# First block of a three-block fp32 transformer kernel: the low parts of weight quarters one batch later, the forget gates' logarithm and the value tiles in another order and other PSUM banks, squares added on VectorE

## The chip, the cores and the metric
One core of a Trainium2 chip runs the whole program. The metric is device time in microseconds (us) of one execution. A trace is taken of one further execution; its span, from the first to the last instruction, is a little shorter than its device time.

## The reference, cut to what matters
512 tokens with 16 meta tokens ahead of them go through one first block and two hybrid layers, all in float32. The change is in the first block:

```python
hn = rms_norm(h, ln_pre_mix)                     # (528, 1024)
proj = hn @ w_in
q_a, k_a, v_a, q_b, k_b, v_b, f_b = ...          # 8 heads each, k_a and v_a 2 heads
o_a = swa_sink_attention(q_a, k_a, v_a, sinks, rel_bias)      # window of 128 and the meta tokens, T5 bias
o_b = forgetting_attention(q_b, k_b, v_b, f_b + b_forget)     # logit[t,s] += sum of log sigmoid(f), s < j <= t
h = h + rms_norm(concat(o_a, o_b) @ w_out, ln_post_mix)
hn = rms_norm(h, ln_pre_ffn)
h = h + rms_norm((silu(hn @ w_gate) * (hn @ w_up)) @ w_down, ln_post_ffn)
```

Two hybrid layers (latent attention, two convolution branches, a gated merge) follow and are the longer part of the time.

## The kernel before, in words
**Products in three parts.** Each float32 matrix x is split into a high part (rounded to fp32r) and a low part (the rest), and a product is three matmuls (`mm3`, L602: high*high, low*high and high*low). Weights come as 134 slots of 128 x 2048 numbers (1 MB), loaded in order by the SP queue into three buffers (L480 to L486); a load waits until the slot three before it is used up (`slot_done`). ScalarE writes the high part (`slot_hi`, L1188), VectorE the low part (`slot_lo`, L1635), each either whole or in quarters of 512 columns, and TensorE waits for both (`split_ready`, L613). All helpers for ScalarE's activations record line 1186, VectorE's record L1626 (tensor with tensor), L1630 and L1633.

**Order.** Each engine's order of work is written out by hand, and the engines meet at counting semaphores. The PSUM has eight banks of 512 columns; banks 0 and 1 are handed on by `bank_read` counters (`Fills`, L165; `wait_fill`, L595).

**First norm** (L701 to L706, L1243 to L1256, L1695 to L1722). ScalarE squares the eight tiles of x, VectorE adds them into `acc`, and TensorE sums over partitions with `acc` against a column of ones (`token_sums`, L644). The last two squares are not added but summed by TensorE too (its argument `late`). The root, its reciprocal on a diagonal (`token_roots`) and `spread` (L659) bring the factor to all partitions; VectorE then scales x and splits it.

**Projections of the first block.** Slot 0: keys and values of the windowed part, and the forget logits beside it. Slots 1 and 2: the keys of the forgetting part (`keys_tile`, L683), two tiles a slot in banks 0 and 1 or 2 and 3; between their halves TensorE makes eight rows of the bias table (`bias_row`, L667) in banks 4 and 5, which ScalarE copies to `brow` (L1231); GpSimd writes them to DRAM and reads them back skewed. Between the two tiles of slot 1 the logits are turned (L739 to L743). VectorE adds the gate's bias (`fx`), ScalarE takes abs, exp(-x) and ln(1+x) (L1294 to L1299, with a load of activation tables before the second and the third), VectorE makes `ls`, and TensorE sums it up by triangular products (L772 to L779). Slots 3 and 4: the values, four tiles of 128 tokens in banks 2 to 5 and one tile of the meta tokens in bank 0 (L754 to L769), copied by VectorE (`v_read`, L1776) and ScalarE (`Vm`, L1312). Slot 5: queries of heads 0 to 3 in banks 0 and 1 (L781), copied to `Qb` by `queries_read`.

**Attention** (L909 to L918). 32 batches: two blocks of 128 queries of one head each, 16 of the forgetting part and then 16 of the windowed part. In iteration j TensorE transposes the probabilities of batch j, does some *dense steps*, then the scores of batch j+2 and the values product of batch j. ScalarE in iteration j: exponentials of j+1, the copy of the transposed batch j, reads of dense tiles, a quarter of a slot's high part (L1372 to L1381). VectorE: norm of j (`normed`), maxima of j+1, and the low part of the same quarter (L1826 to L1836). A dense step is one k of one tile of slots 6 to 10 (3 matmuls of 512 columns): 80 steps in all; `dense_until(j)` (L135) says how many are through after batch j. `SPLITS` (L161) says in which iteration which quarter of slots 7 to 12 is split. Banks 2 to 5 hold scores, 6 and 7 the outputs.

**Second norm** (L924 to L956, L1386 to L1396, L1840 to L1872). Slots 11 and 12 end the output projection in eight tiles; VectorE adds each to `y1` (the trace calls that memory `y`), ScalarE squares it, GpSimd adds up the squares 0 to 6 (`add_up`, L561) between the loads of the adaptation weights that it issues, and TensorE sums and spreads (`token_sums(1, ...)`). Meanwhile slots 13 and 14 (`S_GU`, `S_GU + 1`) are split.

## Time and profile before

| | us |
|---|---|
| median of 3 runs (1864.39 to 1869.49) | 1867.81 |
| the profiled execution: its own time | 1867.15 |
| its span | 1865.2 |
| mean granted TensorE clock | 0.979 of full |
| HBM traffic, mean over the span | 94 GB/s |

TensorE's busy time stands in the rows below. Engines are PE (TensorE), PEld (its weight loads, beside PE), DVE (VectorE), ACT (ScalarE), POOL (GpSimd) and SP (the DMA queue). Times of rows are microseconds from the start of the span, unless marked ns. A matmul row's duration reaches beyond the start of the next one, since they are pipelined; the distance of two starts is what one costs.

### The profile page before, as it was taken

The page shows a single profiled execution, that of the slowest core. Times are in us where ns is not written, and L with a number is a line of the kernel's source. Part 1 is how long each engine was busy: PE and PEld are TensorE (multiplying, and loading weights), DVE is VectorE, ACT ScalarE, POOL GpSimd, SP SyncE. Part 2 cuts the span into 40 slices and gives each one's busy share as a digit, 9 for nine tenths or more (in the row PEclk, how much of TensorE's full clock was granted, in tenths as well). Part 3 has the DMA queues.
Part 4 walks back from the last instruction along what each step waited for, and adds up shares of the span by engine and source line. Part 5 has one row for each costly group of instructions (what it writes and reads, how often), then busy time and mean ns, then how long its engine had stood idle before and what let it go on. Part 6 is the DMA issues. An engine that isn't in the chain of part 4 may idle for free.

```text
span 1865.2 us, 20425 instructions
## 1 busy us (share of the span) xinstructions
PE 1783.6 (96%) x8186; PEld 1425.2 (76%) x8186; DVE 1062.8 (57%) x1724; ACT 689.0 (37%) x1056; POOL 117.1 (6%) x120
## 2 busy tenths in 40 slices
PE   8999998999999999999899999999999999999996
PEld 7766766788888887777788788777777778788775
DVE  6344443776665336634368766557543458766555
ACT  4425454422222234464423322532455422322432
POOL 2100001011000000100000000021100000000002
PEclk8999999999999999999999999999999999999998
DMA  4220012265554321211122222221321112222221
GB/s 163 106 102 24 23 46 82 85 208 204 200 181 164 130 91 68 90 69 68 46 90 91 90 91 103 78 90 46 113 91 49 65 68 91 90 91 90 91 90 46
DMA packets 29532, 177.40 MB, mean 95 GB/s; under 512 B 3613, under 2 KB 3757, under 8 KB 12286
## 3 DMA queue, kind: packets, MB, share of 16 engines
q1 hardware_dynamic: 20448, 144.71, 21.6%
q0 software_dynamic: 8608, 31.21, 4.8%
q8 instruction: 64, 1.05, 0.2%
q10 hardware_dynamic: 382, 0.19, 0.0%
q14 instruction: 30, 0.25, 0.0%
HBM read 171.28 MB, written 4.78 MB: 94 GB/s over the span
## 4 chain that ended last, share of the span: by engine, by line
PE 72%; DVE 6%; ACT 3%; issue 1%; POOL 1%; DMA 0%; DVEq 0%; POOLq 0%
PE ps L603 22%; PE ps L605 22%; PE ps L604 22%; PE ps L1106 2%; PE ps L1091 2%; DVE w_lo L1626 2%; DVE h L1626 1%; PE ps L1097 1%; DVE R L1670 1%; ACT w_hi L1186 1%; POOL acc L524 1%; ACT h L1186 1%; DVE cacc L1633 1%; DVE tmp L1626 0%; DVE ps L2024 0%
## 5 line engine op out<-in xcount | busy, mean ns | idle before, releaser
L603 PE MATMUL ps<-Xh,w_hi 128*128 128x512 f32 (+1 forms) x1664 | 657.0, 395 | 23.8 <-DVE w_lo L1626 9.3
L604 PE MATMUL ps<-Xl,w_hi 128*128 128x512 f32 (+1 forms) x1664 | 642.5, 386 | 0.0
L605 PE MATMUL ps<-Xh,w_lo 128*128 128x512 f32 (+1 forms) x1664 | 642.4, 386 | 0.0
L1626 DVE TENSOR_TENSOR w_lo<-w_raw,w_hi 128x2048 fp32r<-128x2048 f32 (+1 forms) x161 | 312.4, 1942 | 348.8 <-ACT w_hi L1186 348.8
L603 PEld LDWEIGHTS ps<-Xh,w_hi 128*128 128x128 f32 x1664 | 315.4, 190 | 99.2 <-issue 24.4
L1186 ACT ACTIVATE w_hi<-w_raw 128x2048 fp32r<-128x2048 f32 (+1 forms) x155 | 259.7, 1678 | 304.8 <-DMA w_raw<-in_w 278.6
L604 PEld LDWEIGHTS ps<-Xl,w_hi 128*128 128x128 f32 x1664 | 315.7, 190 | 65.3 <-issue 4.8
L605 PEld LDWEIGHTS ps<-Xh,w_lo 128*128 128x128 f32 x1664 | 315.4, 190 | 63.2
L1633 DVE SCALAR_TENSOR_TENSOR cacc<-ain,vec,cacc 128x512 f32<-128x512 f32 x240 | 161.9, 748 | 0.0
L1186 ACT ACTIVATE gt<-ps 128x512 f32<-128x512 f32 x48 | 28.2, 597 | 205.4 <-PE ps L605 205.3
L605 PE MATMUL ps<-act_h,w_lo 128*128 128x512 f32 x176 | 70.2, 399 | 0.0
L604 PE MATMUL ps<-act_l,w_hi 128*128 128x512 f32 x176 | 69.4, 394 | 0.0
L603 PE MATMUL ps<-act_h,w_hi 128*128 128x512 f32 x176 | 69.0, 392 | 0.0
L1186 ACT ACT_TABLE_LOAD x52 | 66.7, 1283 | 3.9 <-issue 3.0
L1186 ACT ACTIVATE Pc<-ps,nmax 128x128 f32<-128x128 f32 (+1 forms) x64 | 33.8, 528 | 60.7 <-DVE nmax L2024 59.6
L1885 DVE CUSTOM_DVE_ANT_0 ada_prod<-ada_w,cact 128x1024 f32<-128x1024 f32 x44 | 53.8, 1223 | 0.1
L1186 ACT ACTIVATE btmp<-ps 128x512 f32<-128x512 f32 x16 | 9.6, 600 | 119.0 <-PE ps L605 119.0
L1106 PE MATMUL ps<-PTc,Vc 128*64 128x128 f32 x320 | 42.6, 293 | 5.7 <-DVE tmp L1626 2.9
L1106 PEld LDWEIGHTS ps<-PTc,Vc 128*64 128x64 f32 x320 | 38.8, 149 | 11.0 <-issue 7.3
L2024 DVE CUSTOM_DVE_ANT_0 ps<-ps,mask 128x128 f32<-128x128 f32 (+1 forms) x64 | 31.4, 499 | 25.5 <-PE ps L1091 24.8
L1186 ACT ACTIVATE Pr<-ps,nmax 128x144 f32<-128x144 f32 (+1 forms) x64 | 31.1, 491 | 39.8 <-DVE nmax L1799 39.8
L1626 DVE TENSOR_TENSOR ain<-sq,ps 128x512 f32<-128x512 f32 x8 | 5.5, 688 | 65.2 <-PE ps L605 65.2
(306 smaller groups left out, 2158.9 us busy)
## 6 DMA issues: line engine op xcount, KB each, us to landing
w_raw<-in_w SPq DMA_DIRECT2D x134, 1024.0 KB, 4.8
ada_w<-in_w_ada POOLq DMA_DIRECT2D x48, 512.0 KB, 4.7
bias_scratch<-brow POOLq DMA_DIRECT2D x2, 1312.0 KB, 6.4
h<-in_xT SPq DMA_DIRECT2D x4, 512.0 KB, 5.7
out<-h SPq DMA_DIRECT2D x4, 512.0 KB, 2.6
bias<-bias_scratch POOLq DMA_DIRECT2D x1, 1024.0 KB, 6.8
bias<-bias_scratch POOLq DMA_DIRECT2D x1, 512.0 KB, 5.0
cact<-in_c POOLq DMA_DIRECT2D x1, 512.0 KB, 6.8
```

The lines of the kernel that those rows point to most:

```text
L524: nc.gpsimd.tensor_tensor(acc[:, :], acc[:, :], src, ALU.add).then_inc(sq_added, 1)
L603: nc.tensor.matmul(o_, whi, xhi, start=start, stop=False)
L604: nc.tensor.matmul(o_, whi, xlo, start=False, stop=False)
L605: return nc.tensor.matmul(o_, wlo, xhi, start=False, stop=stop)
L1091: nc.tensor.matmul(bank(2 + b, P * (b + 1)), Q[:, hd, b * P:(b + 1) * P], K[:, hd, 0:P * (b + 1)], start=True, stop=True).then_inc(s2_full, 1)
L1097: last = nc.tensor.transpose(bank(2 + b, P, c0=P * k), Pc[:, P * (tri(b) + k):P * (tri(b) + k + 1)], ident[:, :])
L1106: last = nc.tensor.matmul(bank(B_O, P, DH * (hd % 2), DH * (hd % 2 + 1), c0=P * b), Vc[:, k, DH * hd:DH * (hd + 1)], PTc[:, P * (tri(b) + ...
L1186: return nc.scalar.activation(o_, i_, f, **kw)
L1626: return nc.vector.tensor_tensor(o_, a_, b_, op)
L1633: return nc.vector.scalar_tensor_tensor(o_, a_, s_, b_, op0, op1)
L1885: nc.vector.tensor_tensor_reduce(prod, ada_w[:, par, :], cact[:, :], 1.0, 0.0, ALU.mult, ALU.add, ada_sum[:, par:par + 1]).then_inc(ada_do ...
L2024: nc.vector.tensor_tensor_reduce(bank(2 + b, n), bank(2 + b, n), mask[:, NM + 384 - P * b:NM + 384 + P], 1.0, 3e38, ALU.add, ALU.min, nmax ...
```

## The change
Nothing is added to or taken from what is computed. In the order of the kernel:
- In the first norm VectorE adds all eight squares; TensorE has eight more warm-up products ahead of the sum.
- The wait for the transposed values and the bias tables is moved from ahead of the first key tile into `bias_row(0)`.
- ScalarE takes the forget gates' logarithm behind bias row 1 in place of behind bias row 3 and slot 3's high part; VectorE's low part of slot 3 goes behind `ls`.
- The value tiles go to banks 0 to 3 and the meta tile to bank 4; banks 2 and 3 are waited for at the third tile, and bias row 7 at the meta tile. Slot 5's tiles wait for the copies of value tiles 0 and 1 and not for the meta tile's.
- The first scores wait for queries of heads 0 and 1 alone; scores of batch 4 wait for heads 2 and 3.
- Slot 7 is split whole ahead of the attention; the quarters of slot 8 begin in batch 2. Low parts are taken one iteration behind the high parts. `dense_until` spreads the steps evenly over all batches.
- In the second norm VectorE adds the squares between the adds of y. Slot 14's high part goes behind square 4 in place of square 6, its low part behind y 5. TensorE has two filler products ahead of the sum.

```diff
@@ -134,12 +134,7 @@
-    q2 = KD * Q2_TILES
-    if j < 0:
-        return FIRST_STEPS
-    if j < 6:
-        return FIRST_STEPS + (j + 1) * (q2 - FIRST_STEPS) // 6
-    return q2 + -(-(j - 5) * (DENSE_STEPS - q2) // (BATCHES - 6))
+    return FIRST_STEPS + -(-(j + 1) * (DENSE_STEPS - FIRST_STEPS) // BATCHES)
@@ -158,7 +153,7 @@
-SPLITS = {j0 + k: (g, k) for j0, g in ((0, 7), (4, 8), (9, 9), (15, 10), (22, 11), (27, 12)) for k in range(4)}
+SPLITS = {j0 + k: (g, k) for j0, g in ((2, 8), (9, 9), (15, 10), (22, 11), (27, 12)) for k in range(4)}
@@ -557,10 +552,6 @@
-
-            add_up(KD, 1, squares(0, KD - 1, KD))
-            pool.wait_ge(sum_full, 2)
-            pool.sem_inc(sq_added, 1)
             for t in range(2, LAYERS * 24):
@@ -592,9 +583,9 @@
         def _(pe):
-            def wait_fill(fills, b):
-
-                v = fills.f[b].val()
+            def wait_fill(fills, b, lag=0):
+
+                v = fills.f[b].val(-lag)
                 if not (isinstance(v, int) and v == 0):
@@ -617,8 +608,8 @@
-            def pair_tile(g, j, fills, xwait=None, xh=Xh[:, :, :], xl=Xl[:, :, :]):
-                wait_fill(fills, j)
+            def pair_tile(g, j, fills, xwait=None, xh=Xh[:, :, :], xl=Xl[:, :, :], lag=0):
+                wait_fill(fills, j, lag)
                 for k in range(KD):
@@ -668,6 +659,9 @@
                     pe.wait_ge(brow_done, hd)
+                else:
+                    pe.wait_ge(v_read, 1)
+                    pe.wait_ge(tabb_done, 1)
                 for o_, c in ((bank(4, ROW_W), slice(0, ROW_W)), (bank(5, ROW_M), slice(ROW_W, ROW))):
@@ -701,7 +695,8 @@
             nc.tensor.matmul(bank(B_O, NM), ones[:, :], accm[:, :], start=True, stop=True).then_inc(meta_full, 1)
-            token_sums(0, KD - 2, (KD - 2, KD - 1), B_ST)
+            warm_up(8, 4)
+            token_sums(0, KD, (), B_ST)
             warm_up(2, 4)
@@ -732,8 +727,6 @@
             split_ready(1)
-            pe.wait_ge(v_read, 1)
-            pe.wait_ge(tabb_done, 1)
             keys_tile(1, 0, 0)
@@ -745,27 +738,26 @@
             keys_tile(2, 1, 6)
-            pe.wait_ge(brow_done, HEADS)
-
-            for b in range(2):
-                pe.wait_ge(bank_read[b], fills.f[b].val())
-            pe.wait_ge(v_read, 1)
-            wait_fill(fills, 0)
             for g in (3, 4):
...
                 for t in range(NB):
+                    if g == 3 and t % 2 == 0:
+                        pe.wait_ge(bank_read[t // 2], fills.f[t // 2].val())
                     for kk in range(4):
...
                         c = slice(NM + t * P, NM + (t + 1) * P)
-                        last = mm3(bank(2 + t), Xh1[:, k, c], Xl1[:, k, c],
+                        last = mm3(bank(t), Xh1[:, k, c], Xl1[:, k, c],
                                    whi, wlo, k == 0, k == KD - 1)
...
                         last.then_inc(tile_full, 1)
+                if g == 3:
+                    pe.wait_ge(brow_done, HEADS)
+                    fills.take(0)
                 for kk in range(4):
...
                     whi, wlo = w(g, kk * T, T)
-                    last = mm3(bank(0, T, 0, NM), Xh1[:, k, 0:NM], Xl1[:, k, 0:NM], whi, wlo, k == 0, k == KD - 1)
+                    last = mm3(bank(4, T, 0, NM), Xh1[:, k, 0:NM], Xl1[:, k, 0:NM], whi, wlo, k == 0, k == KD - 1)
                 last.then_inc(slot_done, 1)
@@ -780,7 +772,8 @@
             for j in range(2):
-                pair_tile(5, j, fills, None, Xh1[:, :, NM:NM + T], Xl1[:, :, NM:NM + T]
+                pe.wait_ge(v_read, 2 + j)
+                pair_tile(5, j, fills, None, Xh1[:, :, NM:NM + T], Xl1[:, :, NM:NM + T], 1 - j
                           ).then_inc(tile_full if j == 0 else slot_done, 1)
@@ -814,6 +807,8 @@
                     pe.wait_ge(pt_done, j - 1)
+                if j == 4:
+                    pe.wait_ge(bank_read[1], q1_fill)
                 if j == FOX_BATCHES // 2:
@@ -901,8 +896,8 @@
             pe.wait_ge(v_read, 1 + NB)
-            for b in range(2):
-                pe.wait_ge(bank_read[b], fills.f[b].val())
+            pe.wait_ge(bank_read[0], fills.f[0].val())
+            q1_fill = fills.f[1].val()
             scores(0)
@@ -950,6 +945,7 @@
+            keep_busy(2, bank(B_O), T)
             token_sums(1, 2 * KD - 1, (KD - 1,), B_ST)
@@ -1286,17 +1282,16 @@
             bias_row(1)
-            bias_row(2)
-            keys_read(1, 1)
-            bias_row(3)
-            slot_hi(3)
-
...
             act_(fa[:, :, :], fa[:, :, :], ACT.Ln, bias=ones[:, 0:1]).then_inc(f_log, 1)
+            bias_row(2)
+            keys_read(1, 1)
+            bias_row(3)
+            slot_hi(3)
             bias_row(4)
@@ -1309,7 +1304,7 @@
             sc.wait_ge(slot_done, 5)
-            act_(Vm[0:NM, P:P + T], bank(0, T, 0, NM), ACT.Copy).then_inc(bank_read[0], 1)
+            act_(Vm[0:NM, P:P + T], bank(4, T, 0, NM), ACT.Copy).then_inc(bank_read[0], 1)
@@ -1321,6 +1316,8 @@
                 queries_read(2 * j, j)
+                if j == 0:
+                    slot_hi(7)
@@ -1391,7 +1388,7 @@
                         slot_hi(S_GU)
-                    if n == KD - 2:
+                    if n == 4:
                         slot_hi(S_GU + 1)
@@ -1692,7 +1689,7 @@
-            for j in range(1, KD - 2):
+            for j in range(1, KD):
                 ve.wait_ge(sq_ready, j + 1)
@@ -1713,7 +1710,6 @@
             ve.wait_ge(r_spread, 1)
-            ve.sem_inc(sq_added, 2)
             for j in range(KD):
@@ -1741,7 +1737,6 @@
             nc.vector.memset(Kb[64:66, :, :], 1.0)
-            slot_lo(3)
@@ -1750,6 +1745,7 @@
             stt(ls[:, :, :], fx[:, :, :], 0.0, fa[:, :, :], ALU.min, ALU.subtract).then_inc(ls_done, 1)
+            slot_lo(3)
             slot_lo(4)
@@ -1776,11 +1772,12 @@
                 ve.wait_ge(tile_full, 1 + 3 + t)
-                nc.vector.tensor_copy(V[:, t, P:P + T], bank(2 + t)).then_inc(v_read, 1)
+                nc.vector.tensor_copy(V[:, t, P:P + T], bank(t)).then_inc(v_read, 1)
             ve.wait_ge(rope_done, 1)
...
             slot_lo(6)
+            slot_lo(7)
@@ -1830,11 +1827,21 @@
                     maxima(j + 1)
-                if j in SPLITS:
-                    slot_lo(*SPLITS[j])
+                if j - 1 in SPLITS:
+                    slot_lo(*SPLITS[j - 1])
                 if j % 4 == 1 and j > 4:
...
+
+            def add_y_square(j):
+
+                ve.wait_ge(sq_ready, KD + j + 1)
+                if j == 1:
+                    ve.wait_ge(sum_full, 1)
+                    tt(acc[:, :], sq[:, 0, :], sq[:, 1, :], ALU.add).then_inc(sq_added, 2)
+                else:
+                    ve.wait_ge(sq_added, KD + j)
+                    tt(acc[:, :], acc[:, :], sq[:, j % 2, :], ALU.add).then_inc(sq_added, 1)
@@ -1842,9 +1849,12 @@
                     tt(y1[:, n, :], bank(j), y1[:, n, :], ALU.add).then_inc(bank_read[j % 2], 1)
+                    if n > 1:
+                        add_y_square(n - 1)
                     if n == 2:
                         slot_lo(S_GU)
-            slot_lo(S_GU + 1)
+                    if n == 5:
+                        slot_lo(S_GU + 1)
@@ -1862,6 +1872,7 @@
             token_roots(1)
+            ve.sem_inc(sq_added, 1)
             ve.wait_ge(r_spread, 2)
...
```

## Rows read from the trace of the kernel before

**Rows 1.** The page: span, and TensorE's busy time (its share) xinstructions

```profile
span 1865.2 us, 20425 instructions
...
PE   1783.6 (96%) x8186; PEld 1425.2 (76%) x8186; DVE 1062.8 (57%) x1724; ACT 689.0 (37%) x1056; POOL 117.1 (6%) x120
```

**Rows 2.** What TensorE waited for, whole run: us in total, times, longest us

```profile
PE ps L829 <- DVE Pr L1630: 3.8, 6, 1.3
...
PE ps L650 <- POOL acc L524: 3.3, 1, 3.3
PE ps L672 <- ACT brow L1186: 3.1, 1, 3.1
...
PE ps L799 <- ACT PTm L1186: 2.2, 4, 0.6
...
PE ps L603 <- ACT brow L1186: 1.4, 1, 1.4
PE ps L799 <- ACT Qb L1186: 1.4, 1, 1.4
...
PE ps L603 <- issue: 1.0, 1, 1.0
...
PE ps L603 <- ACT Vm L1186: 0.8, 1, 0.8
```

**Rows 3.** Timeline: start us, us, what [idle before <-releaser]; first norm, last row later

```profile
10.54 1.56 PE L650 MATMUL ps<-ones,acc 128*128 128x1 f32 x8 [3.08 <-DVE acc L1626]
11.97 3.55 PE L655 MATMUL ps<-ones,sq 128*128 128x1 f32 x16
...
7.41 3.08 DVE L1626 TENSOR_TENSOR acc<-acc,sq 128x512 f32<-128x512 f32 x4 [0.39 <-ACT sq L1186]
...
358.03 0.95 PE L650 MATMUL ps<-ones,acc 128*128 128x1 f32 x8
```

**Rows 4.** Timeline of ScalarE around the forget gates' logarithm

```profile
53.64 0.78 ACT L1186 ACTIVATE brow<-ps 128x384 f32<-128x384 f32 x2 [2.92 <-PE ps L673]
...
58.77 1.91 ACT L1186 ACTIVATE w_hi<-w_raw 128x2048 fp32r<-128x2048 f32 x1
63.46 0.24 ACT L1186 ACTIVATE fa<-fx 128x40 f32<-128x40 f32 x1 [2.78 <-DVE fx L1626]
63.72 1.28 ACT L1186 ACT_TABLE_LOAD   x1
...
66.56 0.33 ACT L1186 ACTIVATE fa<-fa,ones 128x40 f32<-128x40 f32 x1
```

**Rows 5.** Timeline of TensorE: the first product of bias rows 5, 6 and 7

```profile
67.60 0.44 PE L672 MATMUL ps<-onehot_r,tabb_hi 33*128 33x384 f32 x1 [3.10 <-ACT brow L1186]
...
73.04 0.44 PE L672 MATMUL ps<-onehot_r,tabb_hi 33*128 33x384 f32 x1
...
76.94 0.44 PE L672 MATMUL ps<-onehot_r,tabb_hi 33*128 33x384 f32 x1
```

**Rows 6.** Window: us, busy of PE, PEld, DVE, ACT, POOL, clock, DMA, GB/s

```profile
80.00:98.00 18.00, 18.00 (x72) 11.35 (x70) 14.13 (x12) 4.82 (x4) 7.23 (x6) 0.93 0.58 188
```

**Rows 7.** The same view over the attention

```profile
126.00:304.00 178.00, 170.04 (x882) 119.82 (x882) 79.42 (x287) 87.75 (x257) 0.00 (x0) 1.00 0.10 36
```

**Rows 8.** Timeline of ScalarE and VectorE, one batch of the attention

```profile
144.64 0.49 ACT L1186 ACTIVATE Pr<-ps,nmax 128x272 f32<-128x272 f32 x1 [2.71 <-DVE nmax L1799]
...
149.85 0.38 ACT L1186 ACTIVATE Pr<-ps,nmax 128x144 f32<-128x144 f32 x1 [2.71 <-DVE nmax L1799]
...
147.18 0.69 DVE L1626 TENSOR_TENSOR w_lo<-w_raw,w_hi 128x512 fp32r<-128x512 f32 x1 [2.57 <-ACT w_hi L1186]
```

**Rows 9.** Second norm: timeline of ScalarE and GpSimd, then the window view

```profile
311.65 1.31 ACT L1186 ACTIVATE sq<-y 128x512 f32<-128x512 f32 x2 [5.01 <-PE ps L605]
...
322.56 5.54 POOL L524 TENSOR_TENSOR acc<-acc,sq 128x512 f32<-128x512 f32 x4 [4.21 <-ACT sq L1186]
...
328.00:339.00 11.00, 9.77 (x33) 6.88 (x34) 6.99 (x12) 2.72 (x6) 0.10 (x1) 0.69 0.09 36
```

## The prediction

> **What bounds the kernel now.** I read the page's busy times first. TensorE is busy for 1783.6 of 1865.2 us [rows 1], so only its remaining 82 us, and what a low clock costs it, can be won. I then asked for everything that TensorE waits for [rows 2]. The waits that the change can reach all lie in the first 340 us: 3.3 us for the last sum of squares on GpSimd, 3.1 us and 1.4 us for bias rows copied by ScalarE, 1.4 us for Qb, 1.0 us that the view calls issue, 0.8 us for Vm, and in the first block's attention 3.8 us for normed probabilities (Pr) and 2.2 us for PTm. I then read each of these places in order of time. Everything behind 363 us is left as it is, and I expect it to move forward as one piece.
>
> Times below are those of the trace of before. I carry each saving on to the next place and ask there whether something that did not move with it becomes late.
>
> **1. First norm.** Six squares are added on VectorE and two more are summed by TensorE directly: 16 pieces in 3.55 us, behind the 8 pieces of acc, 1.56 us from 10.54 [rows 3]. After the change two further adds run on VectorE. Four such adds took 3.08 us, 0.77 each [rows 3], and acc of square 5 ends at 10.49. Square 7 waits for that add and takes 0.6 by the same timeline, so it ends at 11.2 and the last add at 12.0. Then 1.56 us of sums end at 13.6, where they ended at 15.5: **2.0 us less**. The small work behind the adds on VectorE (wf_lo, Rm, eight Xf pieces, 1.7 us) ends at 13.7, just in time for the reciprocal; that caps the gain, and so do the halves of w_lo between the diagonal and the first Xf. The eight new warm-up products are issued after 7.5, with nothing behind them until 12.0, and cost nothing; if they took until 12.0 the cap would still be there. Bounds: 1.2 us (if the clock rises later than the first real product, as it may since it is low from about 11 to 21 us) and 3.0 us (if the warm-up keeps it high: the same 8 pieces took 0.95 us at full clock [rows 3]).
>
> **2. Value transposes.** The wait for v_read and the tables moves from ahead of the first key tile to bias_row(0), 3.1 us into it. V and Vm are read out during those 3.1 us. The 1.0 us "issue" wait [rows 2] goes: **1.0 us** (0.9 to 1.0).
>
> **3. Forget gates.** ScalarE copies bias row 3, splits slot 3 (1.91 us from 58.77), then waits 2.78 us for fx, because VectorE takes the low part of slot 3 first; Abs, two table loads and Exp and Ln follow from 63.46 to 66.89, and only then bias row 4 [rows 4]. TensorE stands from 64.5 to 67.60. The logits are transposed right behind bias row 1, so after the change the block starts when ScalarE has copied that row, at 50.7: it was idle from there 2.92 us, to the copy of row 2 at 53.64 [rows 4]. The block takes 3.3 us, so that copy is 0.4 us late and ends at 54.9; TensorE asks for it at 56.6. Slot 3's halves are split at the same time as now and needed at 73. So the 3.1 us goes whole. With it goes a stretch at half clock: from one bias product to the next took 5.44 us (67.60 to 73.04) and then, for the same work at full clock, 3.90 us (73.04 to 76.94) [rows 5]: 1.5 us. Together **4.6 us** (3.1 to 4.7).
> The table loads are taken at 1.28 us each, back to back with the activations around them [rows 4]. The Trainium skill, "ScalarE: Activation LUTs", section "What ACT_TABLE_LOAD costs", has 1283 ns and a drain of some 1380 ns behind it for each switch. By an estimate from that page the block would take 6.0 us, row 3's product would wait about 0.9 us, and the sum would be 19.7 in place of 20.6; the rows of this case show no such drain.
>
> **4. Value tiles in banks 0 to 3, the meta tile in bank 4.** Before, all of slot 3 waited until bias row 7 had been copied (1.43 us of idle, 1.4 in [rows 2]). Now tiles 0 and 1 need only banks 0 and 1, long read, and run 5.6 us; banks 2, 3 and 4 are read within 1.4 us. The clock was 0.93 of full in 80 to 98 us [rows 6]: 2.5 us at half, with 0.8 us more before 80, cost 1.6 us. **2.9 us** (1.4 to 3.0). The first of these value tiles is now held up by nothing else: slot 3's low part ends at 63. VectorE's chain behind it (slots 4 and 5, the angles, cum, the ones rows of Qb) depends on the load of slot 5, which is issued when slot 2 is through and so moves too; I find V tiles 0 and 1 copied 6 us before slot 5's tiles want their banks.
>
> **5. Slot 5.** It no longer waits for the copy of Vm [rows 2]: **0.9 us** with the restart. Scores 0 to 3 need only heads 0 and 1, so they no longer wait for the second copy to Qb [rows 2]: **1.5 us**. ScalarE's high part of slot 7, 1.9 us, falls in the 4 us in which it waited for tile 1. VectorE is idle there. Cover gone, it would cost 1.9 us at most.
>
> **6. Attention.** TensorE is busy 170.04 of the 178 us from 126 to 304 [rows 7], so 8.0 us are open. The reason is in one of its batches [rows 8]: ScalarE sits 2.71 us until VectorE's maximum, and VectorE sits 2.57 us until ScalarE's quarter of w_hi. They take turns: 5.21 us a batch (144.64 to 149.85), of which ScalarE's own work is 5.21 - 2.71 = 2.5 and VectorE's 5.21 - 2.57 = 2.6. Now VectorE splits the quarter of the batch before, which is there already, so both run beside each other. The turn that is left, an estimate from the same batch: maxima 1.1, exponentials 1.15, turned copy 1.05, scores 1.4, signals 0.2, together 4.9 us, while TensorE's own work is 170.04/32 = 5.3 us a batch. The quarters of slot 7 leave batches 0 to 3, and dense steps are spread evenly, 2.28 a batch: five more (0.7 us each) stand in batches 0 to 5 where TensorE idled. Every batch has at least two steps, 1.4 us, to cover the turned copy. In the sliding-window half TensorE's batch is only 4.1 to 4.9 us and the steps are fewer than before (2.28 for 2.46), so I leave 1 us: **6.9 us**, bounds 0 and 8.0. Each slot's last quarter is still split before its first tile: slot 8 by batch 6, needed in 11; slot 9 by 13, needed in 17.
>
> **7. Second norm.** GpSimd's last four adds took 5.54 us and TensorE waited 3.3 us for them [rows 2, 9]. VectorE's cost 0.77. But VectorE has other work: after the copies of y it now has, in one queue, y 2, add 1, low part of 13 (square 1 ends at 313.0 [rows 9], then add 1, square 2, the high part of 1.9 and the low part of 2.3: 318.6), y 3, add 2, y 4, add 3, y 5, add 4, low part of 14, y 6, add 5, y 7, add 6. ScalarE's high part of 14 (1.9 us, as in [rows 4]) is done at 323.1, the low part (2.3) at 325.5, four more operations of 0.65 end at **328.1**, where the sum of before began at 328.15. So a faster engine moves the end by 0.1 us only: 14's low part takes the place of GpSimd. What is left is the clock, 0.69 in 328 to 339 [rows 9]; with two more filler products the idle time falls from 3.3 to 2.3 us. If the clock stays up, sums and spread take 1.9 + 1.05 for 3.4 + 1.9 us, 2.7 us less. I have seen it fall after 1.4 us of idle (77.8 to 79.2), so I take a fall, a little later: **0.8 us**, bounds -1.0 (load of slot 14 late behind the ada loads, which delays both parts of it) and 2.8.
>
> **Sum.** 2.0 + 1.0 + 4.6 + 2.9 + 0.9 + 1.5 + 6.9 + 0.8 = 20.6 us. The profiled execution took 1867.15 us for its span of 1865.2; less 20.6 that is **1846.5 us**. The median of the runs shown is 1867.81, 0.7 above it, which is inside their spread. What a measurement of this kernel can tell from no change is about 0.3%, 5.6 us.
>
> **Rivals.**
> A. Attention stays a chain of ScalarE and VectorE: the two waits in [rows 8] speak against it, since both go, the shorter sliding-window batches for it. Then term 6 is 0: 1853.5 us. 14%.
> B. The clock stays up through the second norm and the start: 2 us and 1 us more: 1843.5. 12%. For it: the added fillers. Against it: the fall after 1.4 us.
> C. The forget block in its new place holds up bias rows 2 and 3, or the loads arriving with bias_scratch hold up slot 5: 2 to 4 us of terms 3 and 4 come back, 1850. 7%. The idle 2.92 us in [rows 4] is against it.
> D. The other side: TensorE's queue holds scores(j+2) behind 2.28 dense steps, 1.6 us, from the first batch on. If these are not beside the turn but in it, the turn is 4.9 + 1.6 = 6.5 us, over 5.3, and 32 batches take 208 us for 178: 1867.15 - 13.7 + 30 = 1883.5. It decides as soon as exponentials of j+1 end after transposes of j are issued. Against it: batches without quarters of before run at TensorE's pace with 2.46 steps. 3%.
> E. The moved waits do nothing, as something not in these views ends them (a load, GpSimd's queue with its four bias copies): 1862 or above. 2%.
> The forecast itself has the other 62%, from 1842 to 1851. The range reaches over A and B: 1840 to 1856; below and above it I leave about 2 in 10. Faster by over 0.3% is the forecast, A, B, C: 0.95; within 0.02; slower 0.03.
>
> **What would show it.** In the profile after: no wait of L672 for brow, clock full from about 19 to 300 us; value tiles starting right behind bias row 7; scores 0 right behind slot 5; in 178 us of attention less than 2 us of idle and the pair "ACT Pr from DVE nmax" and "DVE w_lo from ACT w_hi" far below 2.7 and 2.6 us each; the sum of the second norm still waiting some 2 us, now for VectorE. A span of attention above 175 us, or a new wait of TensorE for w_lo, would prove me wrong.

## The result, and the profile after

The changed kernel takes 1841.98 us (median of 4 runs, 1840.64 to 1844.83), the kernel before beside it 1866.74 (4 runs); the ratio is 0.9869, with a 95% interval of 0.985 to 0.9888. That is 24.8 us less. The forecast was 1846.5 in a range of 1840 to 1856: right in sign and range, and 4.5 us too cautious. The profiled execution took 1841.48 us for a span of 1839.7, 25.5 us less than in [rows 1].

The page of the changed kernel, the counterpart of [rows 1]:

```profile
span 1839.7 us, 20426 instructions
...
PE 1776.3 (97%) x8190; PEld 1421.7 (77%) x8190; DVE 1069.5 (58%) x1729; ACT 691.4 (38%) x1053; POOL 109.6 (6%) x114
```

What TensorE waited for in it (us in total, times, longest), a row of the whole run, then all that is left from 20 to 300 us:

```profile
PE ps L641 <- DVE acc L1623: 5.5, 2, 2.8
```
```profile
PE ps L594 <- DVE Xl L1623: 0.7, 3, 0.4
```

Of [rows 2] the waits for Pr, PTm, brow, Qb, Vm and the "issue" wait are all gone. In the second norm TensorE waited 3.3 us for GpSimd's acc before and waits 2.67 us for VectorE's now (of the 5.5 us; the rest is the first norm's).

Timeline of the start and of the projections (start us, us, what, in brackets the idle time before it and its releaser), which answers to [rows 3 to 5]:

```profile
12.17 1.87 PE L641 MATMUL ps<-ones,acc 128*128 128x1 f32 x8 [2.84 <-DVE acc L1623]
...
15.52 2.08 PE L654 MATMUL ps<-tmp,ones 128*128 128x128 f32 x8 [0.42 <-DVE tmp L1627]
...
19.86 0.39 PE L594 MATMUL ps<-Xh,w_hi 128*128 128x264 f32 x1 [0.36 <-DVE Xl L1623]
...
47.78 0.24 ACT L1182 ACTIVATE fa<-fx 128x40 f32<-128x40 f32 x1
48.04 1.28 ACT L1182 ACT_TABLE_LOAD   x1
...
50.88 0.33 ACT L1182 ACTIVATE fa<-fa,ones 128x40 f32<-128x40 f32 x1
51.12 0.76 ACT L1182 ACTIVATE brow<-ps 128x384 f32<-128x384 f32 x2
...
61.61 0.44 PE L666 MATMUL ps<-onehot_r,tabb_hi 33*128 33x384 f32 x1
...
65.51 0.44 PE L666 MATMUL ps<-onehot_r,tabb_hi 33*128 33x384 f32 x1
...
70.21 0.51 PE L594 MATMUL ps<-w_hi,Xh 128*128 128x512 f32 x1
...
112.69 0.41 PE L792 MATMUL ps<-Kb,Qb 128*128 128x144 f32 x2
```

ScalarE takes the logarithm straight behind row 1, without the 2.78 us of waiting of [rows 4]; bias row 5 starts at 61.61 for 67.60 and row 6 is 3.90 us behind it for 5.44 [rows 5]; the first value tile follows bias row 7 (69.41) after 0.80 us, where 2.30 us lay between them.

The window view over the attention, the counterpart of [rows 7]:

```profile
113.00:281.00 168.00, 168.00 (x886) 121.60 (x886) 78.81 (x283) 90.06 (x257) 0.00 (x0) 1.00 0.11 38
```

And the second norm, the counterpart of [rows 9]:

```profile
286.72 1.37 DVE L1623 TENSOR_TENSOR y<-ps,y 128x512 f32<-128x512 f32 x2 [5.02 <-PE ps L596]
...
299.24 2.29 DVE L1623 TENSOR_TENSOR w_lo<-w_raw,w_hi 128x2048 fp32r<-128x2048 f32 x1 [0.83 <-ACT w_hi L1182]
...
303.99 1.05 PE L641 MATMUL ps<-ones,acc 128*128 128x1 f32 x8 [2.67 <-DVE acc L1623]
```

**Where the time came from.** Each line is the difference of one interval between two starts in the two traces:

| interval | saved, us | forecast |
|---|---|---|
| start to first projection product (21.43, 19.86) | 1.57 | 2.0 |
| to the first key tile (41.50, 38.67) | 1.26 | 1.0 |
| to bias row 6 (73.04, 65.51) | 4.70 | 4.6 |
| to the value tiles (79.24, 70.21), then cumulative products (94.86, 84.30) | 3.03 | 2.9 |
| to slot 5 (113.03, 101.56) and to the first scores (125.76, 112.69) | 0.91 + 1.60 | 0.9 + 1.5 |
| to the first transposes (133.18, 120.02) | 0.09 | 0 |
| attention, to the first add of y (310.88, 286.72): 177.70, now 166.70 | 11.00 | 6.9 |
| second norm, to the next projection (338.90, 313.67) | 1.07 | 0.8 |
| sum | 25.23 | 20.6 |

### The profile page after: what moved, and what is told of

It reads as the page before. It is cut to its first block, busy times and chain, and to the rows that moved or that the text cites. A ratio compares the mean times of both kernels' runs of the same rounds, so it can differ in the third digit from the quotient of the medians.

```text
span 1839.7 us, 20426 instructions
## 1 busy us (share of the span) xinstructions
PE 1776.3 (97%) x8190; PEld 1421.7 (77%) x8190; DVE 1069.5 (58%) x1729; ACT 691.4 (38%) x1053; POOL 109.6 (6%) x114
## 3 DMA queue, kind: packets, MB, share of 16 engines
q8 instruction: 64, 1.05, 0.2%
## 4 chain that ended last, share of the span: by engine, by line
PE 73%; DVE 7%; ACT 3%; issue 1%; POOL 0%; DMA 0%; DVEq 0%; ACTq 0%
PE ps L594 22%; PE ps L596 22%; PE ps L595 22%; PE ps L1102 2%; PE ps L1087 2%; DVE w_lo L1623 2%; PE ps L1093 1%; DVE h L1623 1%; ACT w_hi L1182 1%; DVE R L1667 1%; ACT h L1182 1%; DVE cacc L1630 1%; DVE tmp L1623 0%; DVE ps L2035 0%; POOL acc L519 0%
## 5 line engine op out<-in xcount | busy, mean ns | idle before, releaser
L594 PE MATMUL ps<-Xh,w_hi 128*128 128x512 f32 (+1 forms) x1664 | 656.1, 394 | 20.6 <-DVE w_lo L1623 9.3
```

Source lines behind the costliest of these rows:

```text
L594: nc.tensor.matmul(o_, whi, xhi, start=start, stop=False)
```

## The experiments

The edits are shown against the changed kernel unless said otherwise. "Attention" is the interval from the first transpose of probabilities to the first add of y. They ran in four groups (e1 to e4, e5 to e8, e9 to e11, e12), in each of which the kernel before ran on the same chip: 1868.57, 1867.17, 1865.25 and 1866.40 us in the median.

**e1, low parts in the same batch.**
```diff
-                if j - 1 in SPLITS:
-                    slot_lo(*SPLITS[j - 1])
+                if j in SPLITS:
+                    slot_lo(*SPLITS[j])
```


> The changed kernel with one edit: the low part of a weight quarter is again taken in the same iteration as its high part. Theory (the turn of ScalarE and VectorE sets the pace of attention where a quarter is split in one iteration): both long waits come back, VectorE's for w_hi of some 2.5 us and ScalarE's for nmax of some 2.7 us, in the 20 batches that have a quarter; the time from the first transpose to the first add of y, 166.7 us in the changed kernel, grows by 3 to 9 us, and the whole time with it, to 1845 to 1851 us. Rival (the even spread of the dense steps and slot 7's quarters out of batches 0 to 3 made the gain): that stretch stays under 168 us and the time within 1.5 us of 1842.

1852.35 us (1849.99 to 1854.39), ratio to before 0.9918 (0.9895 to 0.9941). Attention took 176.75 us: 10.05 of the 11.0 us come back, more than I had bounded. Waits of all engines in the attention, in the kernel before, in the changed kernel and in e1:

```profile
DVE w_lo L1626 <- ACT w_hi L1186: 69.6, 24, 5.5
ACT esink L1186 <- DVE nmax L1799: 38.4, 16, 3.1
ACT Pr L1186 <- DVE nmax L1799: 36.8, 14, 3.3
```
```profile
ACT Pr L1182 <- DVE nmax L1796: 31.3, 14, 2.9
ACT esink L1182 <- DVE nmax L1796: 29.3, 16, 3.1
DVE ps L1796 <- PE ps L790: 18.9, 7, 4.1
```
```profile
DVE w_lo L1623 <- ACT w_hi L1182: 57.0, 20, 4.2
```

VectorE's wait for w_hi is there 24 times before, 20 times in e1 (once for each quarter), and not in the changed kernel, where VectorE waits for TensorE's scores instead. That is what a bound TensorE looks like. The rival (even steps did it) falls: with the old low parts, even steps and slot 7 ahead of the attention are worth what e1 keeps, 0.95 us.

**e2, the old step rule.**
```diff
-    return FIRST_STEPS + -(-(j + 1) * (DENSE_STEPS - FIRST_STEPS) // BATCHES)
+    q2 = KD * Q2_TILES
+    if j < 0:
+        return FIRST_STEPS
+    if j < 6:
+        return FIRST_STEPS + (j + 1) * (q2 - FIRST_STEPS) // 6
+    return q2 + -(-(j - 5) * (DENSE_STEPS - q2) // (BATCHES - 6))
```


> The changed kernel with one edit: the old rule for how many dense steps are through after each batch (fewer in batches 0 to 5, more later). Theory (the turn is broken by the late low parts, and the steps only fill what is left): TensorE idles again a little in the first six batches, 0 to 2 us in all, waiting for Pr or PTm; the stretch from the first transpose to the first add of y is 166.7 to 169 us, the time 1842 to 1844. Rival (the steps made the gain): the stretch grows by 4 us or more, the time to 1846 or above.

1844.82 us (1838.74 to 1846.83). Attention took 168.62 us, 1.92 more: beside late low parts the even steps are worth 1.9 us, the late low parts five times that. Batches 0, 2 and 4 of e2 have one dense step in place of two or three, and ahead of their scores stand its only three waits. Timeline of one of them:

```profile
130.77 0.40 PE L601 MATMUL ps<-Xh,w_lo 128*128 128x512 f32 x1
131.51 0.51 PE L797 MATMUL ps<-Kb,Qb 128*128 128x144 f32 x2 [0.34 <-ACT PTm L1187]
```

The view calls 0.34 us idle. But in a row of such products the next one starts 0.23 us after a product's start (130.54 and 130.77 here), though each is drawn 0.40 long. Without the wait the scores would have started at 131.00, so they lost 0.51 us. **A wait of TensorE ahead of scores is shown about 0.17 us too short, and one shorter than that isn't shown.** Ahead of transposes it is 0.07 us (see term 6 below). The Trainium skill, "Perfetto Trace Analysis", section "Tensor Engine Instruction (MATMUL, LD_WEIGHTS)", says that a matmul's reported end is a model, not a measurement; the rows here agree.

**e3, the attention's part alone**, on the kernel before: the new `dense_until`, `SPLITS` without slot 7, slot 7 whole ahead of the attention, and
```diff
-                if j in SPLITS:
-                    slot_lo(*SPLITS[j])
+                if j - 1 in SPLITS:
+                    slot_lo(*SPLITS[j - 1])
```


> The kernel before with the attention's part of the change alone: even dense steps, slot 7 split whole ahead of the attention, low parts one iteration later. Theory (the attention's gain stands by itself and is 11.0 us, of which the trace shows 8.0 as idle time and the rest lies under the modelled ends of the matmuls beside short waits): the stretch from the first transpose to the first add of y falls from 177.7 to 167 us, TensorE waits under 0.5 us in it, and the time is 10 to 11.5 us less than before, some 1856. Rival (3 us of the 11 come from the parts ahead of it, such as scores that wait for two heads only, or loads that arrive earlier): the stretch is 169 to 171 us and the gain 6.5 to 8.5.

Attention took 166.70 us, to the hundredth what it takes in the changed kernel, and TensorE waits for nothing in it: the 11.0 us belong to this part and need nothing of the rest. The rival falls. The load of activation tables behind the second norm starts at 351.68, 11.03 us earlier than before (362.71). The whole time is 1853.52 us (1850.77 to 1855.4), 15.1 less than before and not 10 to 11.5, but the interval of the ratio (0.9905 to 0.9944) reaches from 10.5 to 17.8 us, so it doesn't contradict 11.0. The profiled span is 16.4 less. The other 5.3 us of the two traces lie behind 760 us, in code that is the same in both; see the low clock below.

**e4 and e11, slot 14's low part last.**
```diff
-                    if n == 5:
-                        slot_lo(S_GU + 1)
+            slot_lo(S_GU + 1)
+
             def raw_rest(j):
```


> The changed kernel with one edit: in the second norm VectorE's low part of slot 14 goes behind the last add of the squares. Theory (that low part, 2.29 us in front of the last two tiles, took the place of GpSimd's adds and is all that holds the end): the last add ends at about 301.6 in place of 303.9, TensorE waits under 0.6 us for it behind its fillers, and span and time fall by 2.3 us; if the clock then stays up through sum and spread, by up to 3.4. Rival (the chain from tile 7 through y, its square and the last add holds the end near 303.5, or the low part only delays the reciprocal or the first products with slot 14): under 0.7 us.

> The changed kernel with slot 14's low part behind the last add of the squares, once more, beside the changed kernel on the same chip. Theory (2.36 us of wait and about 0.5 us of low clock gone in the second norm): 2.5 to 3.5 us below the changed kernel's median, plus or minus 1.5 us for the clock elsewhere. Rival (the 4.2 us seen at first were the clock elsewhere): within 1 us of it.

1837.74 us (1837.16 to 1840.09) and, beside the changed kernel (1841.39) on one chip, 1836.14 (1834.04 to 1840.99). The sum of e4 and the projection behind it:

```profile
300.77 1.05 PE L641 MATMUL ps<-ones,acc 128*128 128x1 f32 x8 [0.32 <-DVE acc L1623]
...
309.95 0.47 PE L594 MATMUL ps<-Xh,w_hi 128*128 128x512 f32 x1 [0.36 <-DVE Xl L1630]
```

From the first add of y (285.86) to the sum 14.91 us for 17.27, 2.36 less, as worked out; to the projection 24.09 for 26.95. The wait falls from 2.67 to 0.32 us. Against the changed kernel on the same chip (e10) the gain is 5.2 us, more than the 2.5 to 3.5 expected. The second norm has 3.2 of it in those two profiles (26.45 and 23.20 us; the clock fell in the first and not in the second). Another 2.8 us lie between the loads of activation tables at 336.88 and 1774.65 us (e10), in code that is the same in both, where the clock is low for less time (see the last section).

**e5, the logarithm back behind slot 3's high part.**
```diff
             bias_row(1)
+            bias_row(2)
+            keys_read(1, 1)
+            bias_row(3)
+            slot_hi(3)
             sc.wait_ge(f_biased, 2)
...
             nc.vector.memset(Kb[64:66, :, :], 1.0)
+            slot_lo(3)
...
-            slot_lo(3)
             slot_lo(4)
```


> The changed kernel with one edit: the forget gates' logarithm back behind bias row 3 and slot 3's high part on ScalarE, and slot 3's low part ahead of fx on VectorE. Theory (the old place held up bias row 4, 3.1 us, and the clock fell in that wait): TensorE waits some 3 us for brow at the product of bias row 5, the granted clock falls behind it and costs 1.2 to 1.6 us more, and all that follows is 4.3 to 4.9 us later than in the changed kernel, unless the value tiles take some of it back. Rival (what holds row 4 is the load or the split of slot 3, and the place of the logarithm matters little): under 1.5 us.

```profile
56.95 0.44 PE L666 MATMUL ps<-onehot_r,tabb_hi 33*128 33x384 f32 x1
...
64.03 0.44 PE L666 MATMUL ps<-onehot_r,tabb_hi 33*128 33x384 f32 x1 [3.11 <-ACT brow L1182]
...
69.46 0.44 PE L666 MATMUL ps<-onehot_r,tabb_hi 33*128 33x384 f32 x1
...
73.36 0.44 PE L666 MATMUL ps<-onehot_r,tabb_hi 33*128 33x384 f32 x1
```

These are bias rows 4 to 7. From row 4 to row 7 it takes 16.41 us, in the changed kernel 11.70 (57.71 to 69.41): 4.71 us, the term to a tenth. Wait and half clock (69.46 - 64.03 = 5.43 for 3.90) are both back. One run, 1843.0 us: only 1.5 us above the profiled execution of the changed kernel, since its first norm took 0.75 us less and its parts behind the attention another 2.4 us less, all of it in unedited code.

**e6, the wait for bias row 7 put back.**
```diff
             keys_tile(2, 1, 6)
+            pe.wait_ge(brow_done, HEADS)
```


> The changed kernel with one added wait: TensorE waits for the copy of bias row 7 ahead of the first value tile, as before. Theory (term 4: that wait stood bare for 1.4 us and brought the clock down): a wait of 1.3 to 1.5 us for brow appears, the clock is below full in the 6 us behind it, and all that follows is 2.5 to 3.1 us later. Rival (only the wait itself counts, the low clock had another cause): 1.3 to 1.6 us later, clock at full. Other rival (in the changed kernel ScalarE is ahead and the wait is free): under 0.3 us.

```profile
70.92 0.51 PE L594 MATMUL ps<-w_hi,Xh 128*128 128x512 f32 x1 [1.43 <-ACT brow L1183]
```
```profile
70.50:80.00 9.50, 9.08 (x32) 7.29 (x33) 6.65 (x5) 5.37 (x5) 2.35 (x2) 0.82 0.58 236
```

The first is its timeline, the second its window view from 70.5 to 80 us, with a granted clock of 0.82. From bias row 7 (68.62) to the first scores (114.98) 46.36 us for 43.28: 3.08. A wait of 1.43 us costs twice its length here: the clock is at half from 71.7 to 75.1 us. Term 4 holds, both rivals fall. One run, 1843.65 us.

**e7, without the eight warm-up products.**
```diff
-            warm_up(8, 4)
             token_sums(0, KD, (), B_ST)
```


> The changed kernel without the eight added warm-up products ahead of the first sum. In the changed kernel the first 8 pieces of acc took 1.87 us in one execution and 1.05 us in three others, where the clock fell only behind them; the first spread began at 15.52 and at 14.6 to 14.8. Theory (the warm-up keeps the clock up for these pieces, mostly): without it the 8 pieces take 1.5 to 1.9 us and the first spread begins at 15.3 to 15.7. Rival (it does nothing, chance decides): 1.05 us and 14.6 to 14.8, as in three of the four executions with it.

```profile
12.20 1.87 PE L641 MATMUL ps<-ones,acc 128*128 128x1 f32 x8 [4.68 <-DVE acc L1622]
```

The first spread starts at 15.54, all as in the profile of the changed kernel (1.87; 15.52): in that profile the warm-up shows no effect. One run, 1841.1 us. Of the ten profiles with it, six show 1.05 us and a spread at 14.6 to 14.8, four 1.45 to 1.87 us and 15.3 to 15.6. One profile without it can't tell whether it raises that share.

**e8, the second norm's adds back on GpSimd**, slot 14's parts left where the change put them (the `add_up` call restored, `add_y_square` not called).

> The changed kernel with the adds of the second norm's squares back on GpSimd; slot 14's parts stay where the change put them. Theory (the faster adds alone move nothing, since slot 14's low part stands in front of them): from the first add of y to the first piece of the sum is 17.0 to 18.5 us, beside 17.27 in both kernels, and the time is 0 to 1.5 us above the changed kernel's. Rival (the adds on VectorE are worth what they save on GpSimd, 2 us or more, and something else took it): 19.3 us or more, and the time 2 us or more above.

```profile
299.90 2.44 DVE L1627 TENSOR_TENSOR w_lo<-w_raw,w_hi 128x2048 fp32r<-128x2048 f32 x1 [2.03 <-ACT w_hi L1186]
...
300.39 3.08 POOL L519 TENSOR_TENSOR acc<-acc,sq 128x512 f32<-128x512 f32 x1 [0.19 <-ACT sq L1186]
...
303.74 1.26 POOL L519 TENSOR_TENSOR acc<-acc,sq 128x512 f32<-128x512 f32 x1 [0.27 <-ACT sq L1186]
...
305.06 1.87 PE L645 MATMUL ps<-ones,acc 128*128 128x1 f32 x8 [3.59 <-POOL acc L519]
```

My theory fell. From the first add of y (285.80) to the sum 19.26 us, the 19.3 of the rival, and the median is 1844.46 (1840.46 to 1847.83). GpSimd's add that meets VectorE's split of w_lo takes 3.08 us for the 1.26 of the next one: it ends 1.1 us after the split (302.3), as if it had stood until then. The Trainium skill, "Trainium Architecture — The Big Picture", section "What this means for kernel authors", says that VectorE and GpSimd share a port under an exclusive lock; this pair of rows agrees. In the kernel before, slot 13's split fell into a gap of GpSimd (318.87 to 321.2) and slot 14's began at 327.93, 0.2 us before the last add ended.

**e9, the adds alone**: e4 with slot 14's high part behind square 6 again, so that of the second norm's edits the adds on VectorE and the two fillers stay.

> The changed kernel with both parts of slot 14 back in their old places (high part behind square 6, low part behind the last add), so that of the second norm's edits only the adds on VectorE and the two fillers stay. From the first add of y to the first piece of the sum the trace so far has 17.27 us in both kernels, 19.26 with slot 14's parts moved and the adds on GpSimd, and 14.91 with the adds on VectorE and only the low part back. Theory (two edits that cancel: the adds on VectorE take 2.4 us or so off, slot 14's low part ahead of tile 6 puts as much on; with GpSimd it is the high part ahead of square 5 that costs): 14.9 to 15.2 us to the sum, but the last square waits 1.9 us behind slot 14's high part, so that the sum ends 0.3 to 1.2 us later than with the high part early; the stretch to the first product of the next projection, 26.95 in the changed kernel and 24.1 with only the low part back, is 24.3 to 25.5. Rival (the adds need the high part early, or the edits do not add up): 26 us or more.

```profile
286.82 1.37 DVE L1623 TENSOR_TENSOR y<-ps,y 128x512 f32<-128x512 f32 x2 [5.02 <-PE ps L596]
...
301.26 0.95 PE L641 MATMUL ps<-ones,acc 128*128 128x1 f32 x8
...
309.94 0.47 PE L594 MATMUL ps<-Xh,w_hi 128*128 128x512 f32 x1 [1.13 <-DVE Xl L1630]
```

14.44 us to the sum, with no wait left, and 23.12 to the projection: better than expected; the clock never fell there, and with the clock up e11 has 23.20, so the place of the high part matters little. **1835.66 us (1834.63 to 1838.39), ratio to before 0.9845 (0.983 to 0.9859)**, 5.7 us below the changed kernel on the same chip (1841.39); from e11 (1836.14) it can't be told apart. So edits cancelled: the adds on VectorE, with the two fillers, take 2.8 us off the way to the sum, and slot 14's new places put it back, 2.36 us by the low part (e4) and 0.47 by the high part.

**e10, the changed kernel once more.**

> The changed kernel once more, for a direct comparison on one chip and to see how much the places with a low clock vary. Expected: a median within 1.5 us of 1842, a ratio to the kernel before of 0.985 to 0.989. Its first eight pieces of acc take 1.05 us if the clock stays up for them, as in six of the seven executions with the warm-up, and the first spread then starts 0.7 to 0.9 us earlier than at 15.52. If the granted clock in the parts that the change leaves alone is a matter of chance, the stretches of low clock behind 700 us sit at other places than in the first profile of it; if it follows from the program, at the same.

1841.39 us (1838.94 to 1841.56), ratio 0.987 (0.9855 to 0.9885). Window view of 20 us in part of the second hybrid layer that the change doesn't touch: the changed kernel, e10, e7 and e2 (the column before the last two is the granted clock).

```profile
1290.00:1310.00 20.00, 17.21 (x67) 13.50 (x66) 13.63 (x13) 7.35 (x10) 4.48 (x2) 0.89 0.28 106
```
```profile
1290.00:1310.00 20.00, 17.21 (x67) 13.54 (x67) 13.25 (x13) 7.90 (x11) 4.88 (x2) 0.90 0.29 106
```
```profile
1290.00:1310.00 20.00, 17.21 (x67) 13.50 (x66) 13.64 (x13) 7.21 (x10) 4.33 (x2) 0.89 0.30 106
```
```profile
1290.00:1310.00 20.00, 17.22 (x74) 13.62 (x74) 12.20 (x12) 8.94 (x13) 4.89 (x2) 1.00 0.30 106
```

Three profiles whose starts agree within 0.4 us there have the low clock at the same place; in e2, whose work there lies 1.7 us later, it is missing. Over the whole run all nine low stretches of the changed kernel behind 345 us come again in e10, within 0.5 us; e10 has one more at 681 us and one of the nine in two parts. So they aren't scattered at random, but two traces of one program aren't quite the same either. The eight pieces took 1.79 us in e10 and not 1.05.

**e12, 28 warm-up products**, on e9.
```diff
-            warm_up(8, 4)
+            warm_up(28, 4)
```


> The version with slot 14's parts in their old places and the adds of both norms on VectorE, with 28 in place of 8 warm-up products ahead of the first norm's sum. In the executions so far TensorE has nothing to do from 9.3 to 9.9 us until 12.0 to 12.4; in five of eleven the first eight pieces of the sum then took 1.45 to 1.87 us in place of 1.05, and in all of them the clock was at half for some time between 12 and 20 us. Theory (the idle time ahead of the sum decides, and more products close it): they end near 11, the eight pieces take 1.05 us or less, the first spread starts at 14.6 to 14.8 with the clock up, 8 pieces of it take 1.1 in place of 1.65 to 2.1 us, and the first projection product starts at 17.7 to 18.9 us in place of 19.0 to 20.0; the time is 1 to 2 us below that version's 1835.7. Rival (the clock falls somewhere in the norm whatever is put ahead of the sum, since the stretch up to 19 us has other gaps): it falls at the spread instead and the first projection product starts at 18.9 or later, under 1 us gained. Other side (the products are in the way of the sum): the sum starts later than 12.4.

```profile
13.67 0.95 PE L641 MATMUL ps<-ones,acc 128*128 128x1 f32 x8
...
16.10 1.16 PE L654 MATMUL ps<-tmp,ones 128*128 128x128 f32 x8 [0.93 <-DVE tmp L1627]
...
19.52 0.39 PE L594 MATMUL ps<-Xh,w_hi 128*128 128x264 f32 x1 [0.92 <-DVE Xl L1623]
```

The other side came in: the 28 products run until 13.67 and hold the sum up by 1.35 us. Yet the clock is at full from 8 to 20 us, the spread takes 1.16 us, and the first projection product starts at 19.52, 0.46 earlier than in e9. That is later than the 17.7 to 18.9 of the theory, and later than in the six profiles with eight products whose first pieces ran at full clock (18.90 to 19.18). The median is 1838.12 us (1833.88 to 1841.74, 5 runs), which can't be told from e9's. The 20 further products took 13.67 - 9.41 = 4.26 us, 0.21 each, so by this estimate some 20 in all would end where the adds do; that wasn't run.

## Why the prediction was right, and where not

Sign and range came out, and seven of the eight terms within 0.5 us; 4.1 of the 4.6 us by which the sum was short are term 6. The measured 1841.98 lies at the lower edge of what I gave to the forecast itself (1842 to 1851). e1 to e3 test term 6, e4, e8 and e9 term 7, e5 term 3 and e6 term 4. Terms 1, 2 and 5 and the two fillers of the second norm were not undone by an experiment of their own: e7 takes out the warm-up products of term 1 alone, and for the rest there are only the differences of intervals.

**Terms 2 to 5** (projections) measured 1.26, 4.70, 3.03, 0.91 and 1.60 us for 1.0, 4.6, 2.9, 0.9 and 1.5. e5 and e6 confirm the two large ones by undoing them, wait and clock together. Terms 2 and 5 are larger than the idle time shown, which fits what e2 shows. In this kernel no drain shows behind the table loads: from the first row of the block at 47.78 to the copy behind it at 51.12 are 3.34 us with two loads of 1.28. The Trainium skill, "ScalarE: Activation LUTs", section "What ACT_TABLE_LOAD costs", has such a drain, and the estimate from it was 6.0.

**Term 6** (attention) was mis-sized: 11.0 us for 6.9, and beyond the bound of 8.0. The mechanism was right; e1 and e3 show it alone and whole. The step that failed is the bound, "8.0 us are open", read off the busy time of [rows 7]: the rows hide a part of each wait. Beside the Pr and PTm waits of [rows 2] the attention of the kernel before has these:

```profile
PE ps L807 <- ACT PTm L1186: 1.1, 2, 0.7
PE ps L851 <- ACT PTm L1186: 0.7, 1, 0.7
```

Together they are 13 waits of 7.7 us, for 11.0 us lost. Where the rest goes can be read from e1, since it has the products of the changed kernel in the same order, and the two traces can be laid side by side, product by product. e1 shows 14 waits of 6.8 us. At these its starts fall back by 8.6 us (0.16 us more than shown ahead of each score, 0.07 ahead of each transpose), by another 0.95 at the second product of nine scores behind them (0.105 each), and by 0.5 at places that show no wait: 10.05 in all.

The second step that was off is where the time lay. Of these 10.05 us 7.6 are lost in the sliding-window half, where I had taken 1 us off. The batch of [rows 8] is of the forgetting half, where TensorE's own batches (5.0 to 6.0 us in the changed kernel) are about as long as the turn of 5.2; in the sliding-window half most take 3.3 to 4.9 us, so the turn cost more there. Nor does the turn of 4.9 us that I had estimated for the kernel after bind: two batches in a row take 8.9 us (4.91 and 3.98) without a wait of TensorE. The half has no idle time left.

From the first transpose of one batch to that of the next (us), from batch 15 to the last:

| | |
|---|---|
| before | 5.22 4.67 5.25 5.21 5.63 3.98 5.60 3.98 5.60 4.41 5.85 4.91 5.63 4.28 6.33 4.97 |
| changed | 5.22 3.99 5.60 3.98 4.90 3.98 5.60 3.98 4.91 4.68 4.92 3.97 4.90 4.68 4.91 3.27 |

One detail of my signs was wrong: ScalarE's waits for nmax did not go far below 2.7 us (60.6 us in 30 times, 2.0 each, for 75.2). With TensorE as the bound, VectorE's maxima come late because the scores do. Idle time of an engine that isn't the bound told nothing.

**Term 7** (second norm): 17.27 us from the first add of y to the sum in both kernels, the 0.1 us of difference forecast being 0.00, and 1.07 us by the clock for 0.8. That slot 14's low part took GpSimd's place is shown by e4 and e9. What I had not seen is in e8: with the adds on GpSimd the new places of slot 14 would have cost 2.0 us.

**Term 1**: 1.57 us for 2.0. The sum starts at 12.17, the forecast had 12.0, and its first eight pieces took 1.87 us at half clock; in six other profiles they took 1.05 and the spread came 0.7 to 1.0 us earlier, so that the term is 1.6 or 2.3 to 2.5 by the clock. The first norm of the kernel before varies too: e3, which has it unchanged, reaches the first projection product at 21.01 for 21.43.

Of the rivals, A (attention stays a chain) is what e1 makes of the kernel; C, D and E did not come. B's time (1843.5) is near the measured one, but not for B's reason: the clock fell both in the first norm (at 11.81 us) and in the second (at 305.36).

## What to carry to other kernels

When two engines take turns on halves of one job (here the high and the low part of a weight quarter), let the second take last round's half: one line was worth 10 us. Idle time read off a matmul engine's rows is a lower bound of what a wait costs: here 6.8 us shown stood for 10.05 us lost. And when a stage gets a faster engine, look at what stands in that engine's own queue: here one split in front of the last tiles ate most of the gain; moving it behind them gave 2.4 us on the way to the sum, and 4 to 5 us of whole time with what the clock gave elsewhere.

## What the runs showed of the hardware that was not expected

- The low clock in code that no edit touches moves the time by up to 5 us. From the load of activation tables at 362.71 to the one at 1800.69 (before) the code is the same in all kernels. Half the time at half clock in it is what the clock costs at most:

| trace | this part, us | half the time at half clock, us |
|---|---|---|
| before | 1437.98 | 20.5 |
| e1 | 1437.91 | 20.5 |
| changed kernel, e10 | 1436.92, 1437.77 | 18.8, 20.5 |
| e4, e11 (one program) | 1436.26, 1434.97 | 17.1, 15.4 |
| e3 | 1432.65 | 13.7 |

- What decides the places is open. Counted from that first load they are the same within 0.5 us in before, e1, e9 and e10, whose loads lie up to 29 us apart, and others in e4, although this part begins at 333.80 us in e4 and at 333.76 in e9. Two traces of one program differ as well. So it isn't shown that an edit ahead of this part changes its time; with one or two traces of each kernel that can't be told from the difference between executions. Whole times are no measure of a term of 2 us: the intervals are.
- In the first norm the clock fell in all ten profiles with eight more products, between 11.8 and 14.4 us. TensorE had been idle ahead of the sum for 2.75 to 2.93 us in the four in which it fell before or within the first pieces (to 0.50, the 1.2 GHz level) and for 2.1 to 2.8 us in the six in which it held through them, so the idle time alone doesn't separate them. In e12, without that gap, it didn't fall. In the projections a fall followed on 1.43 us of idle time (e6); in the attention of the kernel before none followed on 1.35 us (ahead of 166.76).
- GpSimd's add of 128 x 512 went from 1.28 to 3.08 us beside a split of w_lo on VectorE (e8).
